# Token halves at the end of normed stages in a two-block mixer kernel

## The reference

```
def hybrid_layer(h, p_i, ...):
    h = h + 0.5 * rmsnorm(swiglu(rmsnorm(h, g[0]), ffn1_gu, ffn1_down), g[1])
    z = rmsnorm(h, g[2]) @ w_in
    o_a, o_b, o_c = hgrn2(z...), sliding_window_attention(z...), spatial_gating(z...)
    h = h + rmsnorm(concat(o_a, o_b, o_c) @ w_out, g[3])
    h = h + 0.5 * rmsnorm(swiglu(rmsnorm(h, g[4]), ffn2_gu, ffn2_down), g[5])
    gate = sigmoid(rmsnorm(h, g[6]) @ ple_gate)
    h = h + rmsnorm((p_i @ ple_proj) * gate, g[7])
```

## Time and profile before

| | us |
|---|---|
| median of three runs | 2710.93 |
| profiled execution, device time | 2705.2 |
| its span | 2703.4 |
| PE busy | 2596.4 (96%) |
| VectorE (DVE) busy | 1120.9 (41%) |
| ScalarE (ACT) busy | 997.9 (37%) |
| POOL busy | 1296.2 (48%) |
| mean granted TensorE clock | 0.986 of 2.4 GHz |

### The profile page before, as it was taken

How to read it: one execution, slowest core, us unless ns; L and a number is a source line. 1 busy time by engine, 2 the same in 40 slices (tenths; PEclk the granted TensorE clock), 3 DMA queues, 4 the chain that set the end, 5 groups by cost and what they waited for, 6 DMA issues and landing times.

```text
span 2703.4 us, 33421 instructions
## 1 busy us (share of the span) xinstructions
PE 2596.4 (96%) x12324; PEld 2080.8 (77%) x12324; DVE 1120.9 (41%) x1680; ACT 997.9 (37%) x1482; POOL 1296.2 (48%) x1664
## 2 busy tenths in 40 slices
PE   6999999999999999899999999999999989999997
PEld 3688777777888877677888877888877767888885
DVE  5588666535221058625221046222028645222025
ACT  5323423524233244444232245222234455232234
POOL 1233467555555444345555454555544344555543
PEclk8999999999999999999999999999999989999998
DMA  6212211132333322112333332333322202333332
GB/s 270 71 55 72 79 45 40 60 115 84 101 98 94 97 92 70 32 63 86 95 101 94 94 94 86 94 97 98 98 88 78 63 24 86 94 96 99 96 96 74
DMA packets 63814, 234.23 MB, mean 87 GB/s; under 512 B 7360, under 2 KB 8000, under 8 KB 63168
## 3 DMA queue, kind: packets, MB, share of 16 engines
q1 hardware_dynamic: 61056, 222.33, 26.2%
q10 hardware_dynamic: 2624, 10.00, 1.0%
HBM read 230.00 MB, written 2.10 MB: 86 GB/s over the span
## 4 chain that ended last, share of the span: by engine, by line
PE 84%; DVE 9%; issue 3%; ACT 2%; POOL 1%; DMA 1%; SPq 0%; DVEq 0%; POOLq 0%; ACTq 0%
PE banks L1881 21%; PE banks L1871 21%; PE banks L1872 21%; PE banks L2221 2%; PE banks L2227 2%; PE banks L2222 2%; DVE tmp L1146 2%; DVE sq_sum L1125 1%; DVE xlo L1153 1%; PE banks L1941 1%; PE banks L2342 1%; DVE h L1149 1%; PE banks L2291 1%; PE banks L2293 1%; PE banks L2292 1%
## 5 line engine op out<-in xcount | busy, mean ns | idle before, releaser
L435 POOL TENSOR_TENSOR wlo<-raw,whi 128x256 fp32r<-128x256 f32 x1584 | 1183.2, 780 | 1262.0 <-ACT whi L538 1261.9
L1871 PE MATMUL banks<-xhi,whi 128*128 128x512 f32 x1920 | 752.5, 392 | 2.3 <-DVE z L1779 2.3
L1872 PE MATMUL banks<-xhi,wlo 128*128 128x512 f32 x1920 | 747.5, 389 | 0.0
L1881 PE MATMUL banks<-xlo,whi 128*128 128x512 f32 x1952 | 735.4, 393 | 10.4 <-DVE xlo L1153 10.3
L538 ACT ACTIVATE whi<-raw 128x1024 fp32r<-128x1024 f32 x396 | 415.1, 1053 | 347.0 <-PE banks L1881 336.6
L1881 PEld LDWEIGHTS banks<-xlo,whi 128*128 128x128 f32 x1952 | 365.2, 188 | 96.7 <-DVE xlo L1153 18.5
L1871 PEld LDWEIGHTS banks<-xhi,whi 128*128 128x128 f32 x1920 | 360.4, 188 | 81.9 <-DVE z L1779 3.1
L1872 PEld LDWEIGHTS banks<-xhi,wlo 128*128 128x128 f32 x1920 | 360.5, 188 | 76.2 <-issue 1.9
L1125 DVE TENSOR_TENSOR sq_sum<-sq_sum,tmp 128x512 f32<-128x512 f32 x110 | 85.2, 774 | 464.6 <-ACT tmp L558 464.6
L1871 PE MATMUL banks<-act_hi,whi 128*128 128x512 f32 x704 | 273.9, 389 | 0.0
L1872 PE MATMUL banks<-act_hi,wlo 128*128 128x512 f32 x704 | 273.9, 389 | 0.0
(11 more groups left out here) (419 smaller groups left out, 3181.3 us busy)
## 6 DMA issues: line engine op xcount, KB each, us to landing
raw<-in_stream SPq DMA_DIRECT2D x396, 512.0 KB, 3.5
ada_raw<-in_stream SPq DMA_DIRECT2D x24, 512.0 KB, 7.3
h<-in_x ACTq DMA_DIRECT2D x2, 2048.0 KB, 12.2
out<-h SPq DMA_DIRECT2D x4, 512.0 KB, 2.6
ctx_raw<-in_ctx ACTq DMA_DIRECT2D x1, 1024.0 KB, 19.6
dft_t<-in_dft_t ACTq DMA_DIRECT2D x1, 1024.0 KB, 5.0
ple_raw<-in_ple ACTq DMA_DIRECT2D x2, 512.0 KB, 3.4
mixpar<-in_mixpar ACTq DMA_DIRECT2D x2, 384.0 KB, 4.2
```

Source lines behind the costliest of these rows:

```text
L435: piece = pool.tensor_tensor(wlo[:, i, s], raw[:, i, s], whi[:, i, s].bitcast(F32), ALU.subtract)
L1871: pe.matmul(acc[acc_of[t]][:], whi[:, u % SLOTS, i], x_h, start=(k == 0), stop=False, skip_group_check=split)
L1872: pe.matmul(acc[acc_of[t]][:], wlo[:, u % SLOTS, i], x_h, start=False, stop=False, skip_group_check=split)
L1881: mm = pe.matmul(acc[acc_of[t]][:], whi[:, u % SLOTS, i], x_l, start=False, stop=(k == k_tiles - 1), skip_group_check=leading and m < leads)
```

## The change

It does the following.

- The last tile of `out1`, `down` and `out2` is computed in two token halves (`last_tile`): all inputs for tokens 0 to 255 into one bank, then all inputs for tokens 256 to 511 into another (`second`). A weight unit counts as used only in the second half. The matmuls with ones over the seven added squares (`first_squares`) come before the last input of the first half, the sum of the last squares of half 0 before input 3 of the second half.
- ScalarE's square, logarithm and exponential of a half (`post_half`) stand at the head of `norm_in`, half by half, and between them the four high parts of half 0 and the casts of the next stage's first units.
- Inputs 0 to 3 (AHEAD) of the next stage run in halves on VectorE, ScalarE and PE, all four of half 0 and then all four of half 1. In `leading`, high matmuls are one input ahead of low ones; the sum of the last squares of half 1 follows the first input's high matmuls of half 0.
- The squares of `h` and their adds come four inputs later; the last four follow the eighth input.
- The pre norm's sum comes in the second tile behind the leading ones, at its first input (in `in2` in the first, at input 2).
- `gu` of the first FFN starts its ring of banks at 2; `out1` ends on banks 0 and 1.

`proj` is not halved. The diff, cut to its core:

```
+AHEAD = 4
@@ accumulators
+        elif name[0] == "gu" and name[2] == 0:
+            ring = 2
+            if (name == "out1" or name[0] in ("down", "out2")) and m == n - 1:
+                second[t] = 1 if name == "out1" else bank[t - 1]
@@ ScalarE
+            def post_half(e):
+                key, name, q, source = post[0]
+                s, dst = half(e), inv_rms[:, half(e)]
+                if e == 0:
+                    act.wait_ge(*after("sq_added", (name, q, KT - 3)))
+                act.activation(tmp[1 + (KT - 1) % 2][:, s], source(e), ACT.Square).then_inc(*done(name, (q, KT - 1, e)))
+                act.wait_ge(*after("summed", (key, e)))
+                act.activation(dst, bank[4 + e][:, 0:HALF], ACT.Ln, scale=1.0 / D, bias=eps).then_inc(*done("log", (key, e)))
+                act.wait_ge(*after("log", (key, e)))
+                act.activation(dst, dst, ACT.Exp, scale=-0.5).then_inc(*done("inverse", (key, e)))
+
+            def norm_in(q, gain):
                 for e in range(2):
+                    post_half(e)
+                    for k in range(AHEAD):
+                        act.wait_ge(*after("h_new", (q, k, e)))
+                        act.activation(xhi[:, k, half(e)], h[:, k, half(e)], ACT.Copy, scale=gain[:, k:k + 1])\
+                            .then_inc(*done("x_high", (q, k, e)))
+                    if e == 0:
+                        high_parts(units_to(q) + SLOTS - 1)
+                if last_copy:
+                    last_copy.pop()()
+                for k in range(AHEAD, KT):
+                    if k == AHEAD:
                         high_parts(units_to(q) + SLOTS)
                     if k == 5:
                         high_parts(units_to(q) + SLOTS + 1)
+                    act.wait_ge(*after("h_new", (q, k)))
+                    act.activation(xhi[:, k], h[:, k], ACT.Copy, scale=gain[:, k:k + 1])\
+                        .then_inc(*done("x_high", (q, k)))
+                    squares("h_sq", q, k - AHEAD, h[:, k - AHEAD])
+                for k in range(KT - AHEAD, KT):
                     squares("h_sq", q, k, h[:, k])
@@ y_out
+                for m in range(KT - 1):
+                    if m == KT - 2:
+                        high_parts(first_block[stage] // UNIT + KT * k // UNIT)
                     tile_ready(stage, m, k)
...
@@ VectorE, boundary
+                for e in range(2):
+                    v.wait_ge(*after("inverse", (post, e)))
+                    for k in range(AHEAD):
+                        renewed(k, half(e), (q_pre, k - 1, e) if k else None, [(q_pre, k, e)] + [(q_pre, k)] * e)
+                        if e == 0 and k == AHEAD - 1 and between:
+                            between()
+                        if k and q_pre != "last":
+                            lower(k - 1, half(e), (q_pre, k - 1, e))
+                    if q_pre != "last":
+                        lower(AHEAD - 1, half(e), (q_pre, AHEAD - 1, e))
+                for k in range(AHEAD, KT + 1):
+                    if k < KT:
+                        renewed(k, slice(0, SEQ), (q_pre, k - 1), [(q_pre, k)])
+                    if k > AHEAD and q_pre != "last":
+                        lower(k - 1, slice(0, SEQ), (q_pre, k - 1))
+                        sq_add("h_sq", q_pre, k - 1 - AHEAD)
+                for k in range(KT - AHEAD, KT) if q_pre != "last" else []:
+                    sq_add("h_sq", q_pre, k)
@@ PE
+            def last_tile(stage, k_tiles, leads, hi, lo, first_squares, sum_half, when):
+                m, t = KT - 1, first_tile[stage] + KT - 1
+                for e in range(2):
+                    freed = earlier_second[t] if e else earlier[t]
+                    if counted and freed is not None:
+                        pe.wait_ge(*bank_free(freed))
+                    for k in range(k_tiles):
+                        if e == 0 and k == k_tiles - 1:
+                            first_squares()
+                        if e and k == when:
+                            sum_half(0)
+                        u, i = place(stage, m, k, k_tiles, leads)
+                        if e == 0 and (i == 0 or k == 0):
+                            pe.wait_ge(unit_split, u + 1 - WHOLE_UNITS)
+                        dst, w_h, w_l = last_half(t, e), whi[:, u % SLOTS, i], wlo[:, u % SLOTS, i]
+                        pe.matmul(dst, w_h, hi(k)[:, half(e)], start=(k == 0), stop=False)
+                        pe.matmul(dst, w_l, hi(k)[:, half(e)], start=False, stop=False)
+                        mm = pe.matmul(dst, w_h, lo(k)[:, half(e)], start=False, stop=(k == k_tiles - 1))
+                        keys = [("unit", u)] * (e and i == UNIT - 1) + [(stage, m, e)] * (k == k_tiles - 1)
+                        if keys:
+                            mm.then_inc(*done("product", *keys))
+
+            def leading(stage, key, sum_half):
+                for e in range(2):
+                    for k in range(AHEAD):
+                        leading_high(stage, key, k, e)
+                        if e == 0 and k == 0 and sum_half:
+                            sum_half(1)
+                        if k:
+                            leading_low(stage, key, k - 1, e)
+                    leading_low(stage, key, AHEAD - 1, e)
+                for k in range(AHEAD, KT):
+                    leading_high(stage, key, k)
+                    if k > AHEAD:
+                        leading_low(stage, key, k - 1)
+                leading_low(stage, key, KT - 1)
...
+                    leading(stage, lambda k: (q, k), sum_half)
+                    amid = ((LEADS, 2) if s == 1 else (LEADS + 1, 0)), lambda: pre_sum(q)
```

More of the change, by code:

```diff
@@ L103, in accumulators @@
 def accumulators(stages):
-    bank, earlier, last, ring = [], [], {}, 0
+    bank, earlier, last, ring, second, earlier_second = [], [], {}, 0, {}, {}
     for name, n, _ in stages:
@@ new lines, in leading_low @@
+            def leading_low(stage, key, k, e=None):
+                s = slice(0, SEQ) if e is None else half(e)
+                pe.wait_ge(*after("x_low", key(k) if e is None else (*key(k), e)))
+                for m in range(LEADS):
+                    t = first_tile[stage] + m
+                    u, i = place(stage, m, k, KT, LEADS)
+                    mm = pe.matmul(acc[acc_of[t]][:, s], whi[:, u % SLOTS, i], xlo[:, k, s], start=False, stop=(k == KT - 1),
+                                   skip_group_check=True)
+                    keys = [("unit", u)] * (e != 0 and i == UNIT - 1) + [(stage, m)] * (k == KT - 1)
+                    if keys:
+                        mm.then_inc(*done("product", *keys))
@@ new lines, in tile_of @@
+            def tile_of(stage, m, k_tiles, leads, hi, lo, waits=None, amid=None):
+                t = first_tile[stage] + m
+                if counted and earlier[t] is not None:
+                    pe.wait_ge(*bank_free(earlier[t]))
+                for k in range(k_tiles):
+                    if amid and amid[0] == (m, k):
+                        amid[1]()
+                    u, i = place(stage, m, k, k_tiles, leads)
+                    if i == 0 or k == 0:
+                        pe.wait_ge(unit_split, u + 1 - WHOLE_UNITS)
+                    dst, w_h, w_l = acc[acc_of[t]][:], whi[:, u % SLOTS, i], wlo[:, u % SLOTS, i]
+                    if waits:
+                        pe.wait_ge(*after(waits[0] + "_high", waits[1](k)))
+                    pe.matmul(dst, w_h, hi(k), start=(k == 0), stop=False)
+                    pe.matmul(dst, w_l, hi(k), start=False, stop=False)
+                    if waits:
+                        pe.wait_ge(*after(waits[0] + "_low", waits[1](k)))
+                    mm = pe.matmul(dst, w_h, lo(k), start=False, stop=(k == k_tiles - 1))
+                    keys = [("unit", u)] * (i == UNIT - 1) + [(stage, m)] * (k == k_tiles - 1)
+                    if keys:
+                        mm.then_inc(*done("product", *keys))
@@ L2433, in _ @@
                         attention(layer)
[L2434 to L2438 removed]
+                        for m in range(KT - 1):
+                            tile_of(("out2", layer), m, KT, 0, x_hi, x_lo, None if m else ("mix", lambda k: (layer, k)))
```

283 lines of the change are left out of this document (132 added, 151 removed).

## The result

| | before | after |
|---|---|---|
| median of the runs | 2710.16 (2706.16 to 2711.71) | 2773.63 (2770.33 to 2775.07) |
| profiled execution, span | 2703.4 | 2773.3 |
| mean granted clock | 0.986 | 0.976 |

The changed kernel is slower: ratio 1.0238, 95% interval 1.0225 to 1.0251, 63.5 us between the medians. Forecast were 2744 and at most 2766. The direction was right, the size was not. The two profiled executions lie at opposite ends: the one before (2705.2) is faster than its four timed runs, the one after (2775.1) the slowest of its four. Sums taken from the two traces, 69.9 us in all, are therefore some 6 us above the difference of the medians.

A forecast was written before the change was run, and what follows sets the result against it. VectorE's sequence, then squares, cast and low part, not PE, set the stretches between stages. Eight places and the end add 34.7, the clock 3: 2705.2 becomes 2743, plus 1 for the median: 2744, range 2710 to 2766 (own 2726 to 2758).

The forecast's parts named there:

- the chain: Between stages up to tile 4: VectorE's sequence, then squares, cast and POOL's low part set the time, not PE.
- late sum: Pre norm's sum behind tile 4's start: 0.86 of PE work in the open; 2.8 per `in2`, 1.4 per `gu`.
- the clock: A drop when PE resumes after idling doubles the first leading step (0.95): 3 us taken, bounds 0 and 7.6.
- meetings with POOL: Stretch up to tile 4: whether POOL's work meets VectorE's, 2.83 or 4.43 per unit, 1.6 per place either way.
- the longer tail: Squares 4 to 7 behind the last high part: eighth `h` to tile 4 takes 9.1 instead of 6.2, 2.9 more.
- four adds less before the eighth `h`: VectorE, inputs 4 to 7: four adds fewer precede the eighth input, at 0.60 each alone.
- 1 (the chain closes): Next unit's low part ready when the second half ends, PE never stops: about -20, 2686; chance 0.09.
- 2: Head start larger than its losses, squares' tail overlapping the leads: +0.5 a place, 2706 to 2715; chance 0.06.
- 3 (clock and collisions at their upper ends, 2763): Clock drops and POOL meeting VectorE at their upper ends: 50 + 7.6, 2763; chance 0.16.
- rival 4: Weight loads don't hide under half matmuls: 680 x 0.188 = +128, 2833; chance 0.01.
- the wait behind `down`: Sign: PE idle about 3 us before the first leading matmul, with POOL's low part as releaser.
- the wait for `wlo`: Sign: tile 4 waiting about 2.5 us for POOL's low part of its weights.

The follow-up runs named there:

- late_sum: Kernel before, with only the pre norm's sum moved to the second tile behind the leading ones (`in2`: the first, input 2): 2724.95 us, ratio 1.0062.
- fill: Changed kernel plus three matmuls of ones, result unused, between the leading tiles and tile 4, where PE waits: 2764.49 us, ratio 1.0208.
- early_casts: Changed kernel with the casts of the next stage's first two units moved ahead of the four high parts' end: 2759.93 us, ratio 1.0189.
- late_squares: Kernel before with the late pre norm's sum and also the squares of `h` and their adds four inputs later: 2745.36 us, ratio 1.0133.
- whole_last: Changed kernel with the last tile of `down` and `out2` in one piece again, `out1` still halved: 2798.5 us, ratio 1.0338.

## Why the prediction was wrong

Up to tile 4 the chain held step by step. T counts from the second half's start; the rows of `down` are those of the first one, 974.00:

| step | forecast | measured |
|---|---|---|
| `down`: sum of half 0 | T+1.07 | T+1.07 |
| PE resumes, first unit there | T+11.5 | T+11.6 |
| sum of half 1 | T+12.45 | T+12.6 |
| VectorE's half 1 | T+14.1 | T+14.6 |
| VectorE idle between the halves | 6.3 | 6.34 |
| eighth `h` | T+29.7 | T+30.7 |
| eighth `h` to tile 4 | 9.1 | 9.3 |
| tile 4 | T+38.7 | T+40.0 |
| `out2`: PE's sum of half 1 | T+8.9 | T+9.0 |
| VectorE's half 1 | T+10.5 | T+11.2 |
| tile 4 | T+35.6 | T+36.8 |
| late sum, per `in2` (late_sum) | 2.8 | 2.9, 3.4 |
| late sum, per `gu` or `gate` (late_sum) | 1.4 | 2.0, 2.1 |

That the idle time of VectorE agrees so well is luck: both its ends came 0.4 to 0.5 late.

The step that failed is **the clock**. It was taken at 3, with 0 and 7.6 as bounds, as eight times the first leading step, the only place where PE was thought to resume after idling. But the same text forecast that tile 4 would wait about 2.5 us for `wlo`, and didn't ask what the clock does behind that wait. There it falls at seven places, on work that nothing hides: 14 us in the trace, and fill, which changes only this, gives back 9 to 11. The bound was therefore wrong, and not only the value in it. For the first leading step itself the 3 was about right. That step takes 1.84 instead of 1.02 behind `out1` and the second and third `down`, and behind both `out2` a sum of 0.6 took 1.22, so that VectorE's half 1 came 0.6 late: together some 4 us.

The second error is spread over the stretch up to tile 4. Tile 4 came 1.0 to 2.4 later than forecast at the eight places, 13 us together (33.2 for 20.1), with those 4 us of clock among them. At the first `down`, 0.5 of the 1.3 was there when VectorE began half 1, and 0.5 more came by the eighth `h`. It is not more meetings with POOL, the term named as unknown: behind `down` and `out2` VectorE has eight slowed operations of 512 columns (1.11 to 1.23) before and after. A third, small one is the late sum: its terms add to 14.0, and late_sum measured 15.8 (18.3 between the two traces).

Taken apart by runs, the loss looks like this: late sum +15.8; late squares +20.4, of which 10.4 is the clock behind the wait; the place of the first two casts 13.7 (early_casts); the halved last tile with one or two inputs in halves +16.4 or +11.3 when all else is taken back. These come from different bases, so that their sum, 61 to 66 beside the 63.5, is no proof. For the late squares the text had 2.9 a place for the longer tail, but four adds less before the eighth `h` (4 x 0.60) against it, 0.5 net; in late_squares tile 4 is 0.8 later behind `out2`, so that part was nearly right without the clock. In whole_last the halved last tile is worth 25 to the change, but only because it hides a cast that the change itself put late.

Rivals: 1 (the chain closes) fell, the cast was late as drawn, and even with it early the stretch did not close. 2 fell: tile 4 was later, not equal. 3 (clock and collisions at their upper ends, 2763) was the nearest in time, right about the clock but 10 too low, and not borne out on the collisions. 4 fell: the changed kernel has half matmuls at 973.75, 973.87 and 974.00, each with its own load of 0.19. The sentence of the Trainium skill, "TensorE: Matmul & The Clock Gate", section "The mechanism", on which rival 4 rests would have each such load in the open; the trace doesn't. The same section also has loads pulled ahead where they go to a background weight buffer, which would fit the trace. Of the signs named, the wait behind `down` came with "issue" and not POOL's low part as its releaser, and the wait for `wlo` was 3.2 to 3.3 where 2.5 was written.

## What to carry to other kernels

Where a change makes TensorE wait for some three microseconds in places where it didn't, as here before tile 4, ask what the work behind the wait costs at the lower clock, at every such place and not only at the first; take it as likely and not as certain. A head start is worth only what the next engine can do before it needs the other half: look first at the casts and squares that stand between the halves in program order. Before a producer is moved forward, look at what runs beside it there; here two chains ended together and each slowed the other. And where one constant moves several things, as `AHEAD` moves halves, squares and casts, a run that changes it does not say which of them cost the time.

## What the runs showed of the hardware

- Three matmuls of ones in a wait kept the clock at 1.00 in tile 4 (2.73 us of the 3.3), and the up to 1.4 us that remained did not bring it down. Waits of 3.2 to 3.3 before tile 4 brought 1.2 GHz at seven of seven places in the changed kernel, at four of six in early_casts and at three of six in whole_last; waits of 3.5 to 4.0 in late_squares at seven of seven. The 2.2 to 2.3 us before the leading tiles did so at four of seven places in the kernel before.
- VectorE's two-input operations of 512 columns take 0.68 to 0.75 alone and 1.11 to 1.23 beside POOL's low parts, while POOL's unit goes from 2.83 to 4.43. The Trainium skill, "SBUF — State Buffer", section "SBUF: two separate sides", has the two share a port that one instruction holds to its end. Alternating by instruction fits both being slowed; no run here separates this from a shared rate.
